# From the output product to the experts and back, rebuilt: a router fed by raw rows, one-hot lists in place of a table, accumulating scatters, and a last norm on VectorE

## The reference, cut to what matters

```python
x = layer_norm(ALPHA * x + m, ln1_g, ln1_b)      # m = mixed @ w_o, ALPHA = 4 ** 0.25
f = hier_moe(x, ...)
x = layer_norm(ALPHA * x + f, ln2_g, ln2_b)

def hier_moe(xt, ...):                            # xt: 512 tokens x 1024
    g_prob = softmax(xt @ w_rg + b_rg)            # 4 groups; the best one is taken
    e_logits = (xt @ w_re + b_re)[group]          # its 8 experts
    top_v, top_i = top_k(e_logits, 2)             # 2 experts per token
    gate = softmax(top_v) * g_prob[group]
    # every (token, expert) pair: (silu(x @ w1[e]) * (x @ w3[e])) @ w2[e] * gate, summed per token
```

## Time and profile before

| what | us |
|---|---|
| median of three runs (lowest, highest) | 3784.74 (3770.16, 3794.91) |
| the profiled execution, its own time | 3777.22 |
| its span, first to last instruction | 3775.9 |
| layer 0: from the end of the last piece of `out2` to the first expert product | 2041.2 to 2119.3 |
| layer 0: from the last scatter to the first product of `odd_proj` | 2708.5 to 2772.4 |
| layer 1: from the end of the last piece of `out2` to the first expert product | 3051.8 to 3129.1 |
| layer 1: from the last scatter to the end | 3718.6 to 3775.9 |

### The profile page before, as it was taken

One profiled execution on the slowest core, in us unless ns is written; L12 is line 12 of the kernel. 1 busy time (PEld: TensorE's weight loads), 2 busy tenths in 40 slices (PEclk: granted clock), 3 DMA queues, 4 the chain that ended last, 5 costly groups with the idle time before them and its releaser, 6 DMA issues. The chain is left out here.

```text
span 3775.9 us, 42138 instructions
## 1 busy us (share of the span) xinstructions
PE 3333.2 (88%) x16616; PEld 2756.3 (73%) x16617; DVE 2268.7 (60%) x3515; ACT 1819.7 (48%) x2691; POOL 255.0 (7%) x282
## 2 busy tenths in 40 slices
PE   8989999999898999997587699999669858999993
PEld 6788778777788778775366588888557847888882
DVE  5655343437655433334544699999553647999995
ACT  3233332333323423323342488888533617888883
POOL 1101000001001000000000111111000101111100
PEclk9988999999989999998798799999889979999996
DMA  4110223212200222221002499988713235889993
GB/s 152 46 53 1 78 79 106 76 66 80 85 2 23 90 89 89 89 77 50 0 23 105 168 372 367 368 359 346 279 45 117 74 136 221 362 361 362 366 369 130
DMA packets 134010, 591.16 MB, mean 157 GB/s; under 512 B 29457, under 2 KB 35473, under 8 KB 108081
## 3 DMA queue, kind: packets, MB, share of 16 engines
q1 hardware_dynamic: 114000, 570.13, 39.1%
q0 software_dynamic: 19808, 18.29, 1.5%
HBM read 598.81 MB, written 39.99 MB: 169 GB/s over the span
## 5 line engine op out<-in xcount | busy, mean ns | idle before, releaser
L188 PE MATMUL ps<-r,r 128*128 128x512 f32 (+4 forms) x10880 | 2547.0, 393 | 64.7 <-DVE r L2194 23.1
L188 PEld LDWEIGHTS ps<-r,r 128*128 128x128 f32 x10880 | 2021.4, 190 | 524.2 <-issue 68.5
L3212 DVE TENSOR_TENSOR r<-mem,r 128x1024 fp32r<-128x1024 f32 x768 | 909.1, 1222 | 100.9 <-ACT r L3160 92.4
L3160 ACT ACTIVATE r<-mem 128x1024 fp32r<-128x1024 f32 x768 | 792.2, 1062 | 197.0 <-PE ps L188 188.6
L692 ACT ACTIVATE r<-mem 128x512 fp32r<-128x512 f32 (+2 forms) x512 | 335.0, 662 | 918.2 <-PE ps L188 914.3
L727 DVE TENSOR_TENSOR r<-mem,r 128x512 fp32r<-128x512 f32 (+1 forms) x272 | 186.0, 689 | 472.6 <-ACT r L692 471.5
L729 DVE SCALAR_TENSOR_TENSOR r<-mem,r 128x512 fp32r<-128x512 f32 (+2 forms) x240 | 167.8, 715 | 262.5 <-ACT r L692 261.1
L188 PE MATMUL ps<-mem 128*128 128x64 f32 (+5 forms) x744 | 138.7, 348 | 34.2 <-DMA mem<-in_nsa_cmp_w 14.9
L535 PE MATMUL ps<-mem 128*128 128x128 f32 x384 | 58.3, 308 | 113.8 <-DVE mem L2248 93.9
L188 PEld LDWEIGHTS ps<-mem 128*128 128x128 f32 x744 | 119.3, 236 | 48.6 <-DMA mem<-in_nsa_cmp_w 15.4
L535 PEld LDWEIGHTS ps<-mem 128*128 128x128 f32 x384 | 50.7, 160 | 122.2 <-issue 99.4
(11 more groups left out here) (337 smaller groups left out, 2910.1 us busy)
## 6 DMA issues: line engine op xcount, KB each, us to landing
mem<-in_w_up SPq DMA_DIRECT2D x80, 2048.0 KB, 17.8
mem<-in_w_down SPq DMA_DIRECT2D x80, 2048.0 KB, 7.9
mem<-in_w_gate SPq DMA_DIRECT2D x64, 2048.0 KB, 12.8
mem<-in_w_in SPq DMA_DIRECT2D x10, 2048.0 KB, 7.9
mem<-in_odd_w_qkv SPq DMA_DIRECT2D x6, 2048.0 KB, 8.1
mem<-in_w_o SPq DMA_DIRECT2D x4, 2048.0 KB, 10.5
mem<-yd SPq DMA_DIRECT2D x8, 1024.0 KB, 8.7
mem<-in_rel SPq DMA_DIRECT2D x16, 512.0 KB, 3.4
```

Source lines behind the costliest of these rows:

```text
L188: r = e.matmul(out, a, b, start=start and i == 0, stop=stop and i == n - 1, skip_group_check=skip)
L3160: act.e.activation(wh, w, ACT.Copy).then_inc(*self.S["ex_wh"](self.l, e, i))
L3212: dve.e.tensor_tensor(wl, w, wh.bitcast(F32), SUB).then_inc(*self.S["ex_wl"](self.l, e, i))
```

## The change

The part between the output product and the end of the layer is written anew.

- **`OutRoute`** takes the place of `Out`, `Norm`, `Turn` and `Router`. Gain and bias of the norm are folded into the router's weights (`GB`, on DVE, with column gains loaded apart), so that the router's product takes the *raw* rows: PE turns each tile and multiplies it between the last pieces of the output product (`pe_blocks`), ACT copies the turned rows, and DVE corrects the 36 logits of each tile by mean and deviation afterwards. The norm itself is off this chain: tile 0 on DVE (two `scalar_tensor_tensor`), tiles 1 to 3 on ACT and then on POOL (a multiplication and an addition of 128x1024 each, L3138 and L3139 of the new kernel). SP stores each normed tile twice, in `xd` and in `xa`.
- **The lists** no longer go through `tab`. DVE makes a one-hot matrix of each pair's slot (eight comparisons with a row of numbers) and PE multiplies it with the one-hot of the experts, times token number and times gate: the product is each expert's list of rows and list of weights. Rank products shrink from 28 to 2, with rounded one-hots.
- **`Overflow`** now stands ahead of `Experts`, waits for the value alone and has its barriers inside the branch that is jumped over.
- **`Experts`**: ACT and DVE split the first four pieces of expert 0 ahead of their wait for the rows. ACT's copy of the result multiplies by the gate (already divided by ALPHA). POOL's scatter *adds* into `xa`, two pairs of a token meet in one row, and so each scatter waits until the one before has landed. The weights of expert 1, which went out with the router's loads, now wait until expert 0's rows are in.
- **`Tail`** takes the place of `Combine`, `Norm` and `Finish`: SP loads X back from `xa` tile by tile (2 MB in four transfers) and DVE alone norms a tile: `bn_stats`, `bn_aggr`, `(x - mean) * gain`, reciprocal, `x * r + bias`, with ACT for the root only. In layer 0 PE, ACT and DVE turn the tiles in the same stage and begin the splits of `odd_proj`; in layer 1 SP stores each tile as it is ready.

```diff
+class OutRoute(Out):
...
+    def sp(self, sp):
...
+        for t in range(4):
+            sp.wait_ge(*self.normed(t))
+            rows = slice(128 * t, 128 * t + 128)
+            sp.e.dma_start(K.xd[rows, :], K.X[:, t, :]).then_inc(*S["d_xd"](l))
+            sp.e.dma_start(K.xa[rows, :], K.X[:, t, :]).then_inc(*S["d_xa"](l))
+        sp.wait_ge("d_gx0", l, 0)
         K.open.add(l)
         K.load_weights(K.names.index(("moe", l, 0, 0)) - 1)
...
+    def pe_blocks(self, pe):
...
+        for j in range(4):
+            for i in range(n - 4, n):
...
+                if i == n - 3:
+                    if j >= 1:
+                        self.pe_turn(pe, j - 1)
+                    if j >= 2:
+                        self.pe_logits(pe, j - 2)
+        self.pe_turn(pe, 3)
+        self.pe_logits(pe, 2)
+        self.pe_logits(pe, 3)
...
         pe.wait_ge("rt_v", l, "ohs")
-        bank = K.bank[1]
-        for t in range(4):
-            mm(pe.e, bank[:, 32 * t:32 * t + 32], [(K.ustr if j == t else K.ones, self.ohs[:, j, :])
-                                                  for j in range(t + 1)])
...
+        pe.e.matmul(K.bank[0][:, 0:128], self.ustr, self.ohs, start=True, stop=True)
+        pe.e.matmul(K.bank[0][:, 128:256], self.ones, self.ohs, start=True, stop=True).then_inc(*S["rt_p"](l, "rank"))
+        pe.wait_ge("rt_v", l, "os")
+        mm(pe.e, K.bank[1][:, 0:64], [(self.OS[:, k, t, :], self.OV[:, k, t, :]) for k in range(2) for t in range(4)]).then_inc(
+            *S["rt_p"](l, "lists"))
...
+        for t in range(4):
+            dve.wait_ge("rt_p", l, "logits", t)
+            dve.then("rt_v", v.scalar_tensor_tensor(lg[:, t, :], self.uv[:, 0:36], self.nmu[:, t:t + 1],
+                                                    K.bank[4 + t][:, 0:36], MUL, ADD))
+            r = v.scalar_tensor_tensor(lg[:, t, :], lg[:, t, :], self.mv[:, t, 1:2], self.uv[:, 36:72], MUL, ADD)
...
+        for k in range(2):
+            for t in range(4):
+                r = v.tensor_scalar(self.OS[:, k, t, :], self.iota, self.rv[:, t, k:k + 1], None, ALU.is_equal)
+        r.then_inc(*S["rt_v"](l, "os"))
...
+    def pool(self, pool):
...
+        for t in range(1, 4):
+            x = K.X[:, t, :]
+            pool.wait_ge("ln_a", sid, t)
+            pool.then("ln_g", pool.e.tensor_tensor(x, x, self.gains.gb, MUL), sid, t)
+            pool.then("ln_b", pool.e.tensor_tensor(x, x, self.gains.bb, ADD), sid, t)
+        pool.wait_ge("rt_v", l, "rows")
+        pool.wait_ge("d_xd", l)
+        for e in range(2):
+            self.gather(pool, e)
...
     def scatter(self, pool, e):
         pool.wait_ge("ex_y", self.l, e, 1)
-        pool.e.indirect_dma_start(self.K.yd[:, :], bass.IndirectOffsetOnAxis(self.R.IDX[:, 0, e:e + 1], 0),
...
+        if e:
+            pool.wait_ge(f"d_ys{1 - e % 2}", self.l, e - 1)
+        pool.e.indirect_dma_start(self.K.xa[:, :], bass.IndirectOffsetOnAxis(self.R.IDX[:, 1, e:e + 1], 0),
+                                  self.YY[e % 2], None, bounds_check=S - 1, oob_is_err=False,
+                                  compute_op=ADD).then_inc(*self.S[f"d_ys{e % 2}"](self.l, e))
...
     def loops(self):
         nc, memu = self.K.nc, self.K.memu
-        nc.all_engine_barrier()
         most = nc.values_load(memu[0:1, 152:153], min_val=0, max_val=512)
         with nc.If(most > CAP):
+            nc.all_engine_barrier()
...
+class Tail(Stage):
...
+        sp.wait_ge("d_ys1", l, NE - 1)
         for t in range(4):
+            sp.e.dma_start(K.X[:, t, :], K.xa[128 * t:128 * t + 128, :]).then_inc(*S[f"d_xl{t}"](l))
...
+        for ph, t in lagged(4, 0, 1):
+            mu, var, x = self.mv[:, t, 0:1], self.mv[:, t, 1:2], K.X[:, t, :]
+            if ph == 0:
+                dve.wait_ge(f"d_xl{t}", self.l)
+                v.bn_stats(self.st[:, t, 0, :], x[:, 0:512])
+                dve.then("ln_v", v.bn_stats(self.st[:, t, 1, :], x[:, 512:1024]))
+                dve.then("ln_v", v.bn_aggr(self.mv[:, t, :], self.st[:, t].rearrange("p k n -> p (k n)")))
+                v.tensor_scalar(var, var, 1.0, 1e-5 / ALPHA ** 2, MUL, ADD).then_inc(*S["ln_v"](sid, t, "var"))
+                dve.then("ln_g", v.scalar_tensor_tensor(x, x, mu, self.gains.gb, SUB, MUL), sid, t)
+            else:
+                dve.wait_ge("ln_a", sid, t, "root")
+                dve.then("ln_v", v.reciprocal(var, var))
+                v.scalar_tensor_tensor(x, x, var, self.gains.bb, MUL, ADD).then_inc(*S["ln_b"](sid, t))
```

More of the change, by code:

```diff
@@ L516, in setup @@
         K = self.K
[L517 to L518 removed]
+        self.hr, self.lr = K.halves(self.hi), K.halves(self.lo)
     def place(self, hs, u):
@@ new lines, in turned, with pe_turn @@
+    def turned(self, t, half):
+        return self.K.bank[2 * (t % 2) + half][:, :].rearrange("p (k n) -> p k n", k=4)
+    def pe_turn(self, pe, t):
+        S = self.S
+        pe.wait_ge("dn_ev_v", self.name, 1, t)
+        pe.wait_ge("rt_v", self.l, "uv")
+        if t >= 2:
+            pe.wait_ge("rt_x", self.l, t - 2, 1)
+        for half in range(2):
+            for k in range(4):
+                c = 128 * (4 * half + k)
+                r = pe.e.transpose(self.turned(t, half)[:, k, :], self.K.X[:, t, c:c + 128], self.K.ident)
+            r.then_inc(*S["rt_p"](self.l, "turn", t, half))
@@ new lines, in pe, with act_turned @@
+        pe.e.matmul(K.bank[0][:, 128:256], self.ones, self.ohs, start=True, stop=True).then_inc(*S["rt_p"](l, "rank"))
+        pe.wait_ge("rt_v", l, "os")
+        mm(pe.e, K.bank[1][:, 0:64], [(self.OS[:, k, t, :], self.OV[:, k, t, :]) for k in range(2) for t in range(4)]).then_inc(
+            *S["rt_p"](l, "lists"))
+    def act_turned(self, act, t):
+        K, S, l = self.K, self.S, self.l
+        if t >= 2:
+            act.wait_ge("rt_p", l, "logits", t - 2)
+        for half in range(2):
+            act.wait_ge("rt_p", l, "turn", t, half)
+            act.e.activation(self.XT[t % 2][:, 4 * half:4 * half + 4, :], self.turned(t, half),
+                             ACT.Copy).then_inc(*S["rt_x"](l, t, half))
@@ L3048, in sp @@
     def sp(self, sp):
+        sp.wait_ge("rt_v", self.l, "weights")
+        self.gains.load(sp)
         self.K.load_weights(self.K.names.index(("moe", self.l, NE - 1, 2)))
@@ L3364, in sp @@
         for t in range(4):
-            sp.e.dma_start(self.YB[:, t], K.yd[256 * t:256 * t + 256, :].rearrange("(p k) n -> p k n", k=2)).then_inc(
-                *self.S["d_yb"](l))
-        self.gains.load(sp)
+            sp.e.dma_start(K.X[:, t, :], K.xa[128 * t:128 * t + 128, :]).then_inc(*S[f"d_xl{t}"](l))
+        if not self.turn:
+            for t in range(4):
+                sp.wait_ge("ln_b", self.name, t)
+                sp.e.dma_start(K.out[0, 128 * t:128 * t + 128, :], K.X[:, t, :]).then_inc(*S["d_out"]("out"))
+            sp.wait_ge("d_out", "out")
@@ L3384 @@
[L3384 to L3390 removed]
+            var = self.mv[:, t, 1:2]
+            act.wait_ge("ln_v", sid, t, "var")
+            act.e.activation(var, var, ACT.Sqrt).then_inc(*S["ln_a"](sid, t, "root"))
+        if self.turn:
+            self.follow.begin_act(act, 3)
+            for u in range(8):
+                self.turn.act_unit(act, u)
```

498 lines of the change are left out of this document (289 added, 209 removed).

## The result

| | before | after |
|---|---|---|
| median, us | 3782.98 (4 runs) | 3679.85 (4 runs) |
| profiled execution, us (span) | 3777.2 (3775.9) | 3685.6 (3684.3) |
| ratio of the times | | 0.972, 95% interval 0.968 to 0.977 |

The change makes the kernel 103 us faster by the medians, 92 by the profiled executions; 119 were forecast (3658). The way in (from the first product of `out2` to the first expert product) and the way out came to within 1 us of the forecast in each layer. The two expert loops, forecast unchanged, became 23 us longer.

The account below looks back on a forecast made before the run. PE was busy throughout the expert loops, so only 276.6 us of serial stretches around them could shrink: 32.4 + 31.6 + 27.8 + 27.3 = 119 us off 3777.2 gives 3658; range 3628 to 3706 with the first two rivals.

Parts of the forecast that it names:

- The way in: Per layer, last piece of `out2` to first expert product: 45.7 us against 78.1 and 77.3, gaining 32.4 and 31.6.
- the way out: Behind the last scatter: 36.1 us against 63.9 in layer 0, 30.0 against 57.3 in layer 1; 27.8 and 27.3 gained.
- PE work ahead of the last piece: Folded-weight, turn and logit products in PE's stream before `out2`'s last piece ends: 48 at 0.13 us, 6.3 us.
- The lists: PE's 8 products making the expert lists, at 0.22 us each: 1.7 us, plus 0.9 for four small DVE operations.
- The lock: Last piece to copy of group logits: GpSimd operations hold VectorE's two-SBUF-operand ones; 15.5 us instead of 4.7, costing 10.8.
- One-hots, gates, slots: Logits' copy to slots, per layer: one-hots 5.5 us, rank products under gate arithmetic 2.2, slot operations 4.0.
- Branch and splits: Before expert 0: value and branch 4 us (0 to 9.2), splits 4.9; gather hidden if the branch takes 2 or more.
- The loop: Expert loops, some 587 us each, stay unchanged; adding scatters add 0.4 us of DMA against 1.3 free per 18.1.
- the forecast's own signs of being wrong: Wrong if loops lengthen or a layer's way in isn't 25 to 45 us shorter; ACT's gate-weight waits expected under 2.
- rival 2: Expert loops under DMA pressure: late gate weights cost about 0.5 us an expert, 31 us in all, 3689; chance 0.18.
- rival 3: POOL's wait between scatters bounds the loop once landing exceeds 17.3 us; landing 20 gives 3825, 23.2 gives 4024; chance 0.09.

## Why the prediction was right, and where it wasn't

- *PE work ahead of the last piece*: 6.3 forecast, 8.0 measured (first product of `out2` to last piece 44.7 before, 52.7 now). The mis-sized part is the count: the rows count instructions, and a plain fp32 product is two of them (a turn of 128x128 is one), so that the folded weights and each tile's logits have 16, not 8. The "64" and "28 products" told of the kernel before are such counts too: 32 and 14 products. The lists show the same, 3.67 against 1.7, at a granted clock of 0.50 (1.2 GHz) from 2068 to 2092.
- *The lock*: mechanism right, size near. 14.0 against 15.5 to the copy; in two of eighteen cases (the nine profiled kernels that keep the norm on GpSimd, two layers each) it was 11.8, as the copy slipped through at the last boundary. Taken away, it gave 7.4 and 7.9 of the 10.8: the floor without it was 6.6 and 6.1, not 4.7, as VectorE's last correction waits 1.1 us for PE, whose logits of the last two tiles (32 instructions) take 3.7 to 4.1 us behind the turns, where the forecast had 1.05 for one tile. This is the wrong count again.
- *One-hots, gates, slots*: 5.5 + 2.2 + 4.0 = 11.7 forecast, 11.5 measured (2068.66 to 2080.13).
- *Branch and splits*: 4 and 4.9 forecast. The branch was 0.85, and then the gather, which I had covered by it, ended the wait; the forecast had counted on this cover only for a branch of 2 us or more. From the lists' last operation to the first product 8.1 us instead of 9.6.
- Errors of both signs nearly cancel, and that is luck: too little for PE's work (1.7) and for the lists (3.67 us for the forecast's 1.7), too much for the lock (1.5) and for branch and splits (1.5). Counted from the first product of `out2`, the way in gained 31.8 and 31.4 us, against 32.4 and 31.6.
- *The way out*: 28.6 and 27.8 gained, against 27.8 and 27.3. The tail's waits have the terms that the forecast gave them.
- *The loop*: **this step failed**. "A doubled scatter adds 0.4 us to DMA engines that have 1.3 us of each 18.1 free" compared shares of busy time, and "Nothing" was the wrong answer. Two of the forecast's own signs of being wrong came: the loops lengthened, and ACT's waits for gate weights are 20.8 us where under 2 were named. POOL's queue did go from 4.3% to 6.1% of the engines in the same 180 us, 0.3 us an expert, well inside what was free; but the gate weights had next to no slack in time (ACT waited for them twice before already, 3.3 us in all), and rival 2 had said so ("just in time already"). Rival 2 came half true: 23 us over the two loops, not 31, and not an even 0.5 us an expert but stalls of up to 3 us in some of them. The runs with plain scatters and with the new order show the two conditions, each of which alone is harmless: adding transfers, and loads issued in the wrong order.
- *The scatter chain as bound* (rival 3): 12.1 us of landing, far below 17.3. Not near.

119.1 forecast; 119.7 gained around the loops, less 23.0 in them is 96.7. The profiled execution shows 91.6: the new one had reached `out2_0` 5.5 us later than the old one, which is the spread of the earlier stages.

The copy L3065 was held like the operations on two SBUF operands, and L766, which reads PSUM, was not. The Trainium skill (SBUF — State Buffer, Who interferes with whom) says that a copy can take the shared ports too, in its two-port modes; the trace agrees that it is held (2.36 us against 0.17), and no row shows its mode. The Trainium skill (Runtime: NRT & Kernel Launch, Instruction fetch mechanics) speaks of a stall at a taken branch; in this trace VectorE's gap at the branch is 0.85 and 0.64 us and taking it out gave no more; no run parts such a stall from the load of the value.

## What to carry to other kernels

Free DMA bandwidth doesn't make a streamed load safe: measure, for each load, its landing against the moment of its use, and issue loads in the order in which buffers come free and data is due. A fault in that order can be free until something else makes transfers a little longer. Elementwise work handed to GpSimd held VectorE's operations on two SBUF tensors, and its copy, until each GpSimd operation ended, so give it only to stretches in which VectorE has no such operation on the critical path, or keep it on VectorE: two passes there took 2.6 us where GpSimd took 4.7. And price a PE stall by what follows it too: 1.9 us of idling made an expert 3.0 us longer, as the granted clock was 0.50 for some 3 us behind it.

## What was not expected of the hardware

- The adding scatter delays other transfers by more than its queue's share says: loops of the changed kernel 9 to 14 us longer at a share of 5.9%, against 1 to 4 us at 6.1 to 6.2% of plain traffic. The last one of layer 0 lands 2.2 us later than the last plain one.
- The branch over the unused code and the load of its value cost 0 to 0.6 us on the path when they were taken out.
- PE's granted clock was 0.50 for some 3 us soon after a wait of 1.9 us (2182.60 to 2184.50), and 1.00 in the 10 us before 2180 and behind 2190.
